# A four-layer trunk on one core: x's and h's two-part buffers each shifted in memory by an unused buffer

## The chip, the cores and the metric

The kernel runs on one core of one Trainium2 chip. The metric is the device time of one execution in microseconds (us). TensorE (PE) multiplies matrices, VectorE (DVE) and ScalarE (ACT) work element by element, GpSimd (POOL) has small jobs, and SyncE (SP) issues the DMAs that bring the weights in.

## What is computed

The reference is a trunk of four layers over 256 tokens of width 1024, all in 32-bit floats:

```
for i in range(DEPTH):                                # 4
    x = x + 0.5 * swiglu(rms_norm(x), gate, up, down) # 1024 -> 2816 -> 1024
    h = rms_norm(x)
    x = x + mixer[i % 3](h)      # fox attention, conv module, diff attention
    x = x + 0.5 * swiglu(rms_norm(x), gate, up, down)
```

swiglu is (silu(h @ w_gate) * (h @ w_up)) @ w_down. There are eight such blocks (called ffn below) and four mixers: fox, conv, diff, fox. All weights are read once; with them some 346 MB come from memory.

## The kernel before

Activations stand transposed: 128 features on the partitions, tokens along the row. A product of 32-bit numbers is made of three products of rounded parts (type float32r): each operand is split into a high part and the low rest, and high x high, high x low and low x high are summed in a PSUM bank.

Weights arrive in blocks of 128 partitions x 2048 floats (8 tiles k of 256 columns, 1024 bytes a tile) in a ring of 5 slots. ACT writes the high part (`split_high`, L468), DVE the low part (`split_low`, L786, in the memory where the block landed), and PE waits for the latter.

In an ffn the moving operand of a matmul has both parts side by side. `on_both` (L1362) streams the 256 high and the 256 low values of one tile of x or h (512 columns) past the high weights, and `on_high` (L1367) streams the 256 high values past the low weights. `both_parts` (L1370) issues, for one half n (128 columns) of the weight tiles: one L1362 for the first k, then L1367 for all k, then L1362 for the rest. Each such pair of matmuls, one L1362 and one L1367, handles one k and one n. Each matmul has its own weight load (LDWEIGHTS, in the rows PEld) of 128 columns, 512 bytes of a row.

- Gate and up: 11 pairs of blocks; each of the 22 blocks has 2 halves of 8 pairs of matmuls, so 352 pairs an ffn and 2816 in all, with x_both moving. x_both is [128, 2, 8, 256]: high tiles, then low tiles 8 KB on.
- Down: 12 blocks of 8, 8 and 6 tiles (`DOWN`), so 4 x 22 x 2 = 176 pairs an ffn and 1408 in all, with h_both moving. h_both is [128, 2, 22, 256]: low tiles 22 KB behind the high ones.
- Mixers: three matmuls of 256 columns (`three_passes`, L1353 to L1355), with x moving (`columns_half`), with x as the stationary operand and the weights moving (`tokens_half`), and with o_high and o_low moving (`rows_block`).

Buffers stand in a partition in the order of their declaration. In the built program the weights' ring starts at byte 16,512 (raw and, over it, w_low), w_high at 57,472, xT at 98,432, x_square at 106,624, x_both at 114,816, h_both at 177,376 (q_raw and u_shifted start there too, since they are alive at other times), o_high at 202,112 and o_low at 210,304. Called *phase* below is a byte address modulo 1024, and *distance* a buffer's phase less the weights'. Both parts of the weights have phase 128, and so has every tile of theirs; every tile of x_both has 128, of h_both 224, of o_high and o_low 384.

Of the kernel before, what the change touches and what calls it, by code (L numbers as in the profile page):

```python
# [14 lines left out]
P = 128  # L15
# [43 lines left out]
def build_trunk(nc, A, out):  # L59
# [12 lines left out]
    with ExitStack() as ctx:  # L72
        def sb(name, shape, dt=F32):
            return ctx.enter_context(nc.sbuf_tensor("sb_" + name, shape, dt))
# [10 lines left out]

        xT = sb("xT", [P, KT, SEQ])
        x_square = sb("x_square", [P, KT, SEQ])
        x_both = sb("x_both", [P, 2, KT, SEQ], F32R)
        x_high, x_low = x_both[:, 0, :, :], x_both[:, 1, :, :]
        square_sum = sb("square_sum", [P, SEQ])  # L90
# [64 lines left out]

        with ExitStack() as during_ffn:
            h_both = during_ffn.enter_context(nc.sbuf_tensor("sb_h_both", [P, 2, FF_TILES, SEQ], F32R))
            gate_part = during_ffn.enter_context(nc.sbuf_tensor("sb_gate_part", [P, 2, SEQ], F32))  # L160
            up_part = during_ffn.enter_context(nc.sbuf_tensor("sb_up_part", [P, 2, SEQ], F32))
# [1697 lines left out]
```

## Time and profile before

| what | value |
|---|---|
| median of 3 runs | 2031.18 us (2028.58 to 2031.52) |
| profiled execution, its own time | 2029.96 us |
| its span, first to last instruction | 2028.2 us |
| PE busy | 1986.3 us, 98% |
| DVE busy | 1425.3 us, 70% |
| ACT busy | 1045.6 us, 52% |
| memory traffic | 350.14 MB, 173 GB/s in the mean |
| granted TensorE clock, mean | 0.998 |

A matmul's end in the trace is modelled and lies past the start of the next, so the mean duration of one is no measure of how fast they follow each other. The pace is read from starts, or from the chain that ended last, which gives the time from one run of matmuls to the next.

### The profile page before, as it was taken

The numbers are of one execution on the slowest core, as the hardware profiler recorded it, in microseconds if no ns is written. First come the engines' busy times: TensorE is split into PE (matmuls) and PEld (weight loads), VectorE is DVE, ScalarE is ACT, GpSimd is POOL, SyncE is SP. The second block draws the span as 40 slices with busy tenths as digits, with TensorE's granted clock in tenths as the row PEclk, the third lists the DMA queues.
The fourth block names the chain that finished last, engine by engine and source line by source line (L and its number), as shares of the span: only waits on it lengthen the run. The fifth ranks groups of instructions, "written<-read, shape, count | busy, mean of one in ns | idle before, by whom it ended". The sixth has DMA issues, their size and how long they took to land.

```text
span 2028.2 us, 29077 instructions
## 1 busy us (share of the span) xinstructions
PE 1986.3 (98%) x12584; PEld 1744.9 (86%) x12584; DVE 1425.3 (70%) x1631; ACT 1045.6 (52%) x1247; POOL 114.2 (6%) x120
## 2 busy tenths in 40 slices
PE   7999999999999998999999999999999999999999
PEld 6888888888888896988888888888888888888887
DVE  7775777876787554776587658887658765778763
ACT  5544556654554344654465455665446545456542
POOL 2000201000200001100000000010010001101000
PEclk9999999999999999999999999999999999999999
DMA  7655433665665583565656553355566555335553
GB/s 226 192 183 178 146 125 121 196 193 176 193 190 186 180 248 88 182 190 183 193 187 192 174 181 125 111 181 187 177 197 187 187 184 171 125 114 177 187 183 109
DMA packets 336365, 350.14 MB, mean 173 GB/s; under 512 B 10077, under 2 KB 331886, under 8 KB 336238
## 3 DMA queue, kind: packets, MB, share of 16 engines
q1 hardware_dynamic: 331742, 343.58, 53.3%
q10 hardware_dynamic: 4496, 4.70, 1.0%
q8 instruction: 99, 1.62, 0.3%
q14 instruction: 28, 0.23, 0.0%
HBM read 346.04 MB, written 2.22 MB: 172 GB/s over the span
## 4 chain that ended last, share of the span: by engine, by line
PE 89%; DVE 5%; ACT 4%; issue 1%; DMA 1%; POOL 1%; ACTq 0%; DVEq 0%; POOLq 0%
PE banks L1362 48%; PE banks L1367 25%; PE banks L1353 4%; PE banks L1354 4%; PE banks L1355 4%; ACT sb_w_high L468 1%; DVE sb_w_low L786 1%; ACT sb_scores L594 1%; PE banks L1565 1%; PE banks L1795 1%; PE banks L1603 1%; DVE sb_neg_max L1053 0%; PE banks L1619 0%; PE banks L1586 0%; PE banks L1714 0%
## 5 line engine op out<-in xcount | busy, mean ns | idle before, releaser
L786 DVE TENSOR_TENSOR sb_w_low<-sb_raw,sb_w_high 128x2048 fp32r<-128x2048 f32 (+1 forms) x332 | 754.1, 2275 | 238.8 <-ACT sb_w_high L468 238.2
L1362 PE MATMUL banks<-sb_x_both,sb_w_high 128*128 128x512 f32 x2816 | 727.5, 394 | 3.4 <-DVE sb_w_low L786 3.4
L468 ACT ACTIVATE sb_w_high<-sb_raw 128x2048 fp32r<-128x2048 f32 (+1 forms) x332 | 618.7, 1867 | 141.2 <-DMA sb_raw<-in_ffn_w_down 112.0
L1362 PEld LDWEIGHTS banks<-sb_x_both,sb_w_high 128*128 128x128 f32 x2816 | 501.4, 189 | 86.1 <-DVE sb_w_low L786 3.8
L1367 PEld LDWEIGHTS banks<-sb_x_both,sb_w_low 128*128 128x128 f32 x2816 | 398.8, 191 | 36.0
L1367 PE MATMUL banks<-sb_x_both,sb_w_low 128*128 128x256 f32 x2816 | 408.6, 283 | 0.0
L1362 PE MATMUL banks<-sb_h_both,sb_w_high 128*128 128x512 f32 x1408 | 360.7, 395 | 0.0
L1362 PEld LDWEIGHTS banks<-sb_h_both,sb_w_high 128*128 128x128 f32 x1408 | 251.7, 188 | 46.6
L1367 PEld LDWEIGHTS banks<-sb_h_both,sb_w_low 128*128 128x128 f32 x1408 | 194.6, 188 | 17.1
L1367 PE MATMUL banks<-sb_h_both,sb_w_low 128*128 128x256 f32 x1408 | 200.3, 282 | 0.0
L486 ACT ACTIVATE sb_x_both<-sb_xT,sb_vec 128x256 fp32r<-128x256 f32 x96 | 43.5, 501 | 207.7 <-DVE sb_xT L819 179.1
L1353 PE MATMUL banks<-sb_x_both,sb_w_high 128*128 128x256 f32 x512 | 148.8, 291 | 0.0
L539 ACT ACTIVATE sb_up_part<-banks 128x512 f32<-128x512 f32 x88 | 52.3, 595 | 182.5 <-PE banks L1362 182.5
L1354 PE MATMUL banks<-sb_x_both,sb_w_high 128*128 128x256 f32 x512 | 144.9, 283 | 0.0
L1355 PE MATMUL banks<-sb_x_both,sb_w_low 128*128 128x256 f32 x512 | 144.8, 283 | 0.0
L539 ACT ACTIVATE sb_gate_part<-banks 128x512 f32<-128x512 f32 x88 | 52.4, 595 | 167.3 <-PE banks L1362 167.3
L952 DVE TENSOR_TENSOR sb_up_part<-banks,sb_up_part 128x512 f32<-128x512 f32 x88 | 60.7, 690 | 64.5 <-ACT sb_up_part L539 64.5
L1353 PEld LDWEIGHTS banks<-sb_x_both,sb_w_high 128*128 128x128 f32 x512 | 98.1, 192 | 3.2 <-issue 3.0
L1354 PEld LDWEIGHTS banks<-sb_x_both,sb_w_high 128*128 128x128 f32 x512 | 98.2, 192 | 1.6 <-issue 1.4
L936 DVE TENSOR_TENSOR sb_gate_part<-banks,sb_gate_part 128x512 f32<-128x512 f32 x88 | 60.7, 690 | 54.5 <-ACT sb_gate_part L539 54.2
L1355 PEld LDWEIGHTS banks<-sb_x_both,sb_w_low 128*128 128x128 f32 x512 | 98.1, 192 | 0.0
L816 DVE SCALAR_TENSOR_TENSOR sb_xT<-banks,sb_xT 128x512 f32<-128x512 f32 x32 | 22.1, 691 | 100.5 <-PE banks L1362 100.5
(210 smaller groups left out, 1957.1 us busy)
## 6 DMA issues: line engine op xcount, KB each, us to landing
sb_raw<-in_ffn_w_gate SPq DMA_DIRECT2D x88, 1024.0 KB, 5.4
sb_raw<-in_ffn_w_up SPq DMA_DIRECT2D x88, 1024.0 KB, 5.4
sb_raw<-in_ffn_w_down SPq DMA_DIRECT2D x64, 1024.0 KB, 5.0
sb_raw<-in_ffn_w_down SPq DMA_DIRECT2D x32, 768.0 KB, 4.3
sb_raw<-in_fox_w_in SPq DMA_DIRECT2D x24, 1024.0 KB, 5.2
sb_raw<-in_conv_w_pw SPq DMA_DIRECT2D x12, 1024.0 KB, 5.4
sb_raw<-in_diff_w_in SPq DMA_DIRECT2D x12, 1024.0 KB, 5.0
sb_raw<-in_fox_w_out SPq DMA_DIRECT2D x8, 1024.0 KB, 5.0
```

Source lines behind the costliest of these rows:

```text
L468: act.activation(slot(w_high, b)[:, 0:width(b)], slot(raw, b)[:, 0:width(b)], ACT.Copy).then_inc(S["high_ready"], 1)
L486: act.activation(x_high[:, t, :], xT[:, t, :], ACT.Copy, scale=vec[:, col + t:col + t + 1]).then_inc(S["xhigh_ready"], 1)
L539: act.activation((up_part if which else gate_part)[:, :, :], banks[:, at:at + 2, SEQ:], ACT.Copy).then_inc(S["up_part_ready" if which else ...
L786: dve.tensor_tensor(slot(w_low, b)[:, 0:width(b)], slot(raw, b)[:, 0:width(b)], slot(w_high, b)[:, 0:width(b)].bitcast(F32), ALU.subtract) ...
L816: dve.scalar_tensor_tensor(xT[:, 2 * T:2 * T + 2, :], sums[:, :, SEQ:], 0.5, xT[:, 2 * T:2 * T + 2, :], ALU.mult, ALU.add).then_inc(S["x_h ...
L936: dve.tensor_tensor(gate_part[:, :, :], banks[:, at:at + 2, 0:SEQ], gate_part[:, :, :], ALU.add).then_inc(S["gate_sum_ready"], 1)
L952: dve.tensor_tensor(up_part[:, :, :], banks[:, at:at + 2, 0:SEQ], up_part[:, :, :], ALU.add).then_inc(S["up_sum_ready"], 1)
L1353: pe.matmul(dst, s_high, m_high, start=first, stop=False, skip_group_check=loose)
L1354: pe.matmul(dst, s_high, m_low, start=False, stop=False, skip_group_check=loose)
L1355: return pe.matmul(dst, s_low, m_high, start=False, stop=last, skip_group_check=loose)
L1362: return pe.matmul(pair(bank[at][:, :]), high[:, n * P:(n + 1) * P], m_both, start=first, stop=last, skip_group_check=True)
L1367: pe.matmul(bank[at][:, SEQ:2 * SEQ], low[:, n * P:(n + 1) * P], m_high, start=False, stop=False, skip_group_check=True)
```

## The change

Two buffers are declared that nothing reads or writes.

```
         x_square = sb("x_square", [P, KT, SEQ])
+        sb("shift_x", [P, 16])
         x_both = sb("x_both", [P, 2, KT, SEQ], F32R)
...
+        sb("shift_h", [P, 200])
         with ExitStack() as during_ffn:
             h_both = during_ffn.enter_context(nc.sbuf_tensor("sb_h_both", [P, 2, FF_TILES, SEQ], F32R))
```

The first takes 16 floats = 64 bytes of each partition, the second 200 floats = 800 bytes. The weights, xT and x_square stay where they are. x_both and what is declared between it and h_both move up by 64 bytes, and h_both and what is declared behind it by 864. No instruction, wait, size or order differs.

## Rows read from the trace of the kernel before

**Rows 1.** Page: busy us by engine, and the granted clock in 40 slices.
```profile
PE 1986.3 (98%) x12584; PEld 1744.9 (86%) x12584; DVE 1425.3 (70%) x1631; ACT 1045.6 (52%) x1247; POOL 114.2 (6%) x120
...
PEclk9999999999999999999999999999999999999999
```

**Rows 2.** Page: the chain that ended last, by engine and by line.
```profile
PE 89%; DVE 5%; ACT 4%; issue 1%; DMA 1%; POOL 1%; ACTq 0%; DVEq 0%; POOLq 0%
PE banks L1362 48%; PE banks L1367 25%; PE banks L1353 4%; PE banks L1354 4%; PE banks L1355 4%; ACT sb_w_high L468 1%; DVE sb_w_low L786 1%; ACT sb_scores L594 1%; PE banks L1565 1%; PE banks L1795 1%; PE banks L1603 1%; DVE sb_neg_max L1053 0%; PE banks L1619 0%; PE banks L1586 0%; PE banks L1714 0%
```

**Rows 3.** Stretches, gate and up and down: PE, PEld, DVE, ACT, POOL, clock, DMA, GB/s.
```profile
836.00:906.00 70.00, 70.00 (x403) 61.62 (x402) 57.88 (x55) 42.11 (x43) 0.00 (x0) 1.00 0.63 199
951.00:1009.00 58.00, 58.00 (x331) 50.56 (x331) 30.72 (x24) 22.22 (x20) 3.70 (x5) 1.00 0.58 185
```

**Rows 4.** PE in order of time, gate and up: start us, length us (last end modelled), what.
```profile
874.00 2.00 PE L1362 MATMUL banks<-sb_x_both,sb_w_high 128*128 128x512 f32 x8
...
929.87 2.00 PE L1362 MATMUL banks<-sb_x_both,sb_w_high 128*128 128x512 f32 x8
```

**Rows 5.** Chain that ended last, 940 to 1010 us: start us, time to the next piece, what.
```profile
941.20 1.84 PE banks L1362 x8
943.04 0.95 PE banks L1367 x8
944.00 1.84 PE banks L1362 x8
...
956.87 0.96 PE banks L1367 x8
957.83 1.87 PE banks L1362 x8
959.70 0.72 PE banks L1367 x6
960.41 1.40 PE banks L1362 x6
```

**Rows 6.** The same chain over the whole span, its longest pieces: same down stage.
```profile
988.92 1.87 PE banks L1362 x8
```

**Rows 7.** PE in order of time: first matmul of a gate-and-up stage, of its down stage, of the next.
```profile
824.90 0.40 PE L1362 MATMUL banks<-sb_x_both,sb_w_high 128*128 128x512 f32 x1
...
948.24 0.40 PE L1362 MATMUL banks<-sb_h_both,sb_w_high 128*128 128x512 f32 x1
...
1010.41 0.39 PE L1362 MATMUL banks<-sb_x_both,sb_w_high 128*128 128x512 f32 x1
```

**Rows 8.** PE in order of time: o moving, 23 matmuls from the first start to the last.
```profile
321.29 0.28 PE L1354 MATMUL banks<-sb_o_low,sb_w_high 128*128 128x256 f32 x1
...
323.91 0.28 PE L1355 MATMUL banks<-sb_o_high,sb_w_low 128*128 128x256 f32 x1
```

**Rows 9.** PE in order of time: weights moving, x stationary, 7 matmuls.
```profile
299.51 0.28 PE L1355 MATMUL banks<-sb_w_high,sb_x_both 128*128 128x256 f32 x1
...
300.22 0.28 PE L1355 MATMUL banks<-sb_w_high,sb_x_both 128*128 128x256 f32 x1
```

**Rows 10.** PE in order of time, half clock, o moving, 10 matmuls.
```profile
799.91 0.42 PE L1355 MATMUL banks<-sb_o_high,sb_w_low 128*128 128x256 f32 x1
...
801.83 0.41 PE L1355 MATMUL banks<-sb_o_high,sb_w_low 128*128 128x256 f32 x1
```

**Rows 11.** Stretches of rows 10 and rows 8: busy us by engine, granted clock, DMA share, GB/s.
```profile
799.50:802.50 3.00, 3.00 (x15) 3.00 (x16) 1.33 (x2) 2.94 (x7) 0.00 (x0) 0.50 0.02 5
321.00:324.00 3.00, 3.00 (x28) 3.00 (x26) 2.76 (x11) 1.32 (x6) 0.00 (x0) 1.00 0.77 270
```

**Rows 12.** Weight loads by line and form, whole span: count, busy us, mean ns.
```profile
L1362 PEld LDWEIGHTS banks<-sb_x_both,sb_w_high 128*128 128x128 f32 x2816 | 501.4, 189 | 86.1 <-DVE sb_w_low L786 3.8
L1367 PEld LDWEIGHTS banks<-sb_x_both,sb_w_low 128*128 128x128 f32 x2816 | 398.8, 191 | 36.0
L1362 PEld LDWEIGHTS banks<-sb_h_both,sb_w_high 128*128 128x128 f32 x1408 | 251.7, 188 | 46.6
L1367 PEld LDWEIGHTS banks<-sb_h_both,sb_w_low 128*128 128x128 f32 x1408 | 194.6, 188 | 17.1
```

More of the change, by code:

```diff
@@ L87, in build_trunk @@
         x_square = sb("x_square", [P, KT, SEQ])
+        sb("shift_x", [P, 16])
         x_both = sb("x_both", [P, 2, KT, SEQ], F32R)
@@ L154, in build_trunk @@
         neg_lam = sb("neg_lam", [P, 1])
+        sb("shift_h", [P, 200])
         with ExitStack() as during_ffn:
```

## Prediction

> **What bounds the kernel now.** I read the page first. PE is busy 98% of the span and the clock is full nearly throughout [rows 1]; the chain of waits that ended last lies on PE for 89%, and 73 of these points are the two matmul lines of the ffn stages [rows 2]. DVE and ACT have room: in a stretch of gate and up PE is busy 70.00 of 70 us, DVE 57.88 and ACT 42.11; in a down stage 58.00 of 58, 30.72 and 22.22, with DMA engines at 0.58 to 0.63 [rows 3]. So in the ffn stages nothing but the pace of PE's own stream sets the time. The change moves data and nothing else; it can act only if that pace hangs on addresses.
>
> So the pace itself has to be read. Gate and up: two runs of eight L1362 start at 874.00 and 929.87 us; a run of eight L1362 and one of eight L1367 take about 2.79 us [rows 4, 5], so 20 such rounds or 160 pairs lie between, 349.2 ns a pair. Down: the same place of a round recurs at 957.83 and 988.92 us [rows 5, 6], two output tiles of 44 pairs apart, so 31.09 us / 88 = 353.3 ns a pair. The whole stages agree: 824.90 to 948.24 us for 352 pairs is 350.4 ns (with the sum of squares and the start in it), and 948.24 to 1010.41 for 176 is 353.2 [rows 7].
>
> The reader is to see that the same two instructions, with the same sizes, go 4.1 ns a pair slower with h moving than with x moving. The chain tells where: eight L1362 take 1.84 us with x and 1.87 with h, six take 1.40 with h (233 ns each against 230), while eight L1367 take 0.95 and 0.96 [rows 5]. DVE and ACT are less busy in the slower stage [rows 3], so it is not they. Three things differ: h stands at distance 96 from the weights and x at 0; h starts at a multiple of 32 bytes (177,376) but not of 64, x at a multiple of 128 (114,816); and h's low part lies 22 KB behind its high part, x's 8 KB.
>
> **What the pace holds beyond the columns.** At half clock (1.2 GHz), 9 starts of 256-column matmuls take 801.83 - 799.91 = 1.92 us, 213.3 ns each, which is 256 columns at that clock and nothing more [rows 10, 11]. At full clock (2.4 GHz) the columns would take half, 106.7 ns; 22 starts with o moving take 2.62 us, 119.1 ns each [rows 8, 11]. So each matmul holds about 12 ns more than its columns. A pair has 768 columns, 320 ns, and takes 349.2 or 353.3: 29 or 33 ns of something else. Part of this might be two streams of reads, the running matmul's data and the next weights, getting into each other's way at certain addresses. That is all that this change could win.
>
> **What the rows say of addresses.** 256-column matmuls go at 119 ns with o at distance 256 [rows 8], at 0.95/8 = 119 with x at distance 0, at 0.96/8 = 120 with h at 96 [rows 5], and at 0.71/6 = 118 with the roles of x and weights exchanged [rows 9]. Weight tiles are read in halves 512 bytes apart, and the chain's runs of eight L1362 with x at one half and at the next take 1.84 us both [rows 5]. So for these four distances the short matmul does not care. Only the 512-column matmul shows a difference, and only for h.
>
> **The change part by part.** No instruction comes or goes, so there is no count to price, only paces.
>
> h_both: 177,376 + 864 = 178,240, phase 64, distance -64. It becomes a multiple of 64 bytes, as x is. My reading is that the start of a row of h off a multiple of 64 makes each 256-value run touch one more unit of memory, which the 512-column matmul, with two such runs, pays and the short one hides. Then h falls to x's pace: 353.3 - 349.2 = 4.1 ns x 1408 pairs = 5.8 us. Bounds: nothing, if the 22 KB or something else is the cause; and more than 5.8 only if distance itself matters (a rival below).
>
> x_both: 114,816 + 64 = 114,880, phase 192, distance 64. Still a multiple of 64, no longer of 128. The trace has nothing at distance 64 or at an odd multiple of 64, so this is the term that I can't read. From both sides: above, x falls to h's pace, +4.1 x 2816 = +11.5 us; below, the 29 ns vanish, -29 x 2816 = -82 us. I take 0, because distances 0 and 256, both multiples of 64, give one pace for the short matmul, and the only deviating buffer is the one that is not such a multiple.
>
> Mixers: x moving there moves by 64, o by 864 to distance 96. Their short matmuls go at 119 at 0 and 256, and h's at 120 at 96: 768 matmuls with o x 0.5 ns is 0.4 us at most. I take 0. What else moves (scores, probabilities, padded conv input, copies that DVE, ACT and POOL read and write) moves by 64 or 864 bytes under operations that lie beside PE's work in all but a few per cent of the chain [rows 2]; 0 as well. If every DVE and ACT piece on the chain, 9% of it, changed by 1%, that would be 1.8 us either way.
>
> Sum: -5.8 us. Against the profiled execution 2028.2 - 5.8 = 2022.4 us of span, its own time 2029.96 - 5.8 = 2024.2; that execution is 1.2 us under the median. From the median of the runs: 2031.2 - 5.8 = **2025.4 us**, -0.29%. What a measurement of this kernel tells from no change is about 0.2%, 4.1 us.
>
> **A rule against it.** L1367's weight loads last 191 ns in the mean beside x and 188 beside h [rows 12], so loads are, if anything, shorter beside the slower stream; the trace alone does not decide whether the two streams meet. The Trainium skill (TensorE: Matmul & The Clock Gate, Step-by-step: what each phase is for) says that PE has two independent read ports and that loading the next weights takes nothing from the running matmul. By that rule distance is nothing, and the sum would be 0 for it. The Trainium skill (SBUF — State Buffer, Door 1: The DMA port swizzle) also says that memory lines are 16 bytes; by that rule an address off 64 but on 32 costs nothing, the sum is 0 again, and no row at a finer offset can show it.
>
> **The rivals.**
>
> *Addresses do nothing.* h's 4.1 ns come of its 22 KB between parts, which stays. For it: one pace at distances 0, 256 and 96 for short matmuls [rows 5, 8]. Against it: nothing in the trace ties 22 KB to a cost either. Time: 2031 us. Chance 0.23. The two rules of the Trainium skill cited above speak for this rival; the second is from its page SBUF — State Buffer.
>
> *x gets slower.* The unit is 128 bytes and not 64, or a small distance that is not 0 costs, as 96 does. x's rows start at 64 past a multiple of 128 and go at h's pace; h stays at its own. Place: every L1362 of gate and up. Price: +4.1 x 2816 = +11.5 us, 2042.7 us, +0.57%. It decides once x loses more than h's 5.8 us / 2816 = 2.1 ns a pair. For it: the only distance between 0 and 256 in the trace is the slow one. Against: the short matmul at 96 is as fast as the others. Chance 0.27.
>
> *The streams come apart.* At 64 bytes from the weights the reads of matmul and weights never meet, and some of the 29 to 33 ns a pair goes. All of it would be 29 x 2816 + 33 x 1408 = 128 us, 1903 us; a sixth of it 21 us, 2010 us. For it: the 12 ns that each matmul holds at full clock and none at half clock [rows 8, 10]. Against: halves of the weight tiles 512 bytes apart are served alike, and 0, 96 and 256 hold the same 12 ns; a meeting that only one distance avoids should show a trace at these. Chance 0.12.
>
> *Other*, such as both streams worse than any shown distance: 0.05, mostly slower.
>
> **How the numbers follow.** My forecast has the remaining 0.33; its own range is 2022 to 2031, since h may keep some of its difference. Of it I count 0.24 as faster by over 0.2% and 0.09 as within. Of the first rival 0.02, 0.19 and 0.02 are faster, within and slower, for scatter between runs. Of x slower, 0.24 slower and 0.03 within, if h gains at the same time (+5.7 net, near the bound). The third rival gives 0.12 faster, the rest 0.01 and 0.04. Sum: faster 0.39, within 0.31, slower 0.30. The range holds forecast, no effect, x slower and the mild part of the third rival: 2012 to 2044 us. It leaves out most of the third rival and what is worse than 2044.
>
> **What would show each step.** In the profile after, down rounds 88 pairs apart by 30.7 us and eight L1362 in 1.84 us, with gate and up still at 2.79 us a round: right as forecast. Down still at 31.09: addresses do nothing for h. Gate and up at 2.83 us a round: x slower. Rounds under 2.75 us in either: streams come apart. PE's busy share stays at 98% in every case. The prediction is wrong if the pace of x moves at all, since twice as many pairs hang on it as on h's.

## The result and the profile after

The changed kernel takes 2008.4 us (median of 4 runs, 2007.77 to 2009.38) against 2030.62 beside it; the ratio is 0.9894, 95% interval 0.9882 to 0.9906. It is 1.06% or some 22 us faster, 3.6 us below the range that was given (2012 to 2044 us).

The page of the changed kernel (busy us by engine; two lines more in the source, so L1362 is L1364 and L1367 is L1369) shows the same bound as [rows 1]: PE busy 98% with 25.8 us less, DVE and ACT unchanged.

```profile
span 2006.3 us, 29077 instructions
...
PE 1960.5 (98%) x12584; PEld 1722.1 (86%) x12584; DVE 1424.5 (71%) x1631; ACT 1045.4 (52%) x1247; POOL 114.2 (6%) x120
```

The first matmuls of a gate-and-up stage, its down stage and the next, changed kernel, answer to [rows 7] (start us, modelled length, what):

```profile
816.38 0.40 PE L1364 MATMUL banks<-sb_x_both,sb_w_high 128*128 128x512 f32 x1
...
938.15 0.40 PE L1364 MATMUL banks<-sb_h_both,sb_w_high 128*128 128x512 f32 x1
...
999.46 0.39 PE L1364 MATMUL banks<-sb_x_both,sb_w_high 128*128 128x512 f32 x1
```

Gate and up takes 121.77 us for 352 pairs, 345.9 ns a pair, where it took 350.4; down takes 61.31 us for 176, 348.3 where it took 353.2. Gate and up is 123.34 - 121.77 = 1.57 us shorter and down 62.17 - 61.31 = 0.86; in eight ffn these are 12.6 us with x and 6.9 us with h, 19.4 us together by the unrounded paces. The span is 2028.2 - 2006.3 = 21.9 us shorter, which leaves some 2.5 us for the rest, the mixers among it. That rest is one profiled execution less another, and ten executions of one kernel lay 4.8 us apart (2026.62 to 2031.38 us, the kernel with everything moved, below), so it is no more than a hint.

The chain that ended last, changed kernel, answers to [rows 5] (start us, time to the next piece, what):

```profile
931.20 1.83 PE banks L1364 x8
933.03 0.94 PE banks L1369 x8
933.97 1.83 PE banks L1364 x8
935.81 0.91 PE banks L1369 x8
936.71 1.83 PE banks L1364 x8
...
947.60 1.86 PE banks L1364 x8
949.46 0.69 PE banks L1369 x6
950.14 1.40 PE banks L1364 x6
```

The reader is to see where the time went out. With x moving (down to 936.71), eight long matmuls lost only 0.01 us, 1.84 to 1.83. Eight short ones went from 0.95 to 0.94 and 0.91 in turn: the two halves of a weight tile, alike before, are now served at different paces. With h moving (from 947.60), six long ones take 1.40 as before and six short ones 0.69 instead of 0.72. Of the 4.5 ns a pair with x and the 4.9 with h, most sits in the short matmuls, of which the prediction said that they do not care.

The weight loads answer to [rows 12] (view of groups by line; count, busy us, mean ns): beside x, the load of low weights is now 188 ns in the mean where it was 191.

```profile
L1369 PEld LDWEIGHTS banks<-sb_x_both,sb_w_low 128*128 128x128 f32 x2816 | 391.2, 188 | 36.8
```

### The profile page after: what moved, and what is told of

It is laid out like the page before. It is cut to its first block, busy times and chain, and to the rows that moved or that the text cites. A ratio compares the mean times of both kernels' runs of the same rounds, so it can differ in the third digit from the quotient of the medians.

```text
span 2006.3 us, 29077 instructions
## 1 busy us (share of the span) xinstructions
PE 1960.5 (98%) x12584; PEld 1722.1 (86%) x12584; DVE 1424.5 (71%) x1631; ACT 1045.4 (52%) x1247; POOL 114.2 (6%) x120
## 4 chain that ended last, share of the span: by engine, by line
PE 88%; DVE 5%; ACT 4%; issue 2%; DMA 1%; POOL 1%; ACTq 0%; DVEq 0%; POOLq 0%
PE banks L1364 48%; PE banks L1369 24%; PE banks L1355 4%; PE banks L1357 4%; PE banks L1356 4%; ACT sb_w_high L470 1%; DVE sb_w_low L788 1%; ACT sb_scores L596 1%; PE banks L1567 1%; PE banks L1797 1%; DVE sb_neg_max L1055 1%; PE banks L1605 0%; PE banks L1716 0%; DVE sb_scores L1048 0%; DMA u_away<-sb_u_pad 0%
## 5 line engine op out<-in xcount | busy, mean ns | idle before, releaser
L1364 PE MATMUL banks<-sb_x_both,sb_w_high 128*128 128x512 f32 x2816 | 723.0, 392 | 3.5 <-DVE sb_w_low L788 3.5
L1364 PEld LDWEIGHTS banks<-sb_x_both,sb_w_high 128*128 128x128 f32 x2816 | 497.7, 188 | 82.9 <-DVE sb_w_low L788 3.9
L1369 PEld LDWEIGHTS banks<-sb_x_both,sb_w_low 128*128 128x128 f32 x2816 | 391.2, 188 | 36.8
L1369 PE MATMUL banks<-sb_x_both,sb_w_low 128*128 128x256 f32 x2816 | 399.5, 278 | 0.0
L1364 PE MATMUL banks<-sb_h_both,sb_w_high 128*128 128x512 f32 x1408 | 360.1, 394 | 0.0
L1364 PEld LDWEIGHTS banks<-sb_h_both,sb_w_high 128*128 128x128 f32 x1408 | 250.2, 188 | 45.7
L1369 PEld LDWEIGHTS banks<-sb_h_both,sb_w_low 128*128 128x128 f32 x1408 | 190.8, 188 | 17.1
L1369 PE MATMUL banks<-sb_h_both,sb_w_low 128*128 128x256 f32 x1408 | 194.3, 279 | 0.0
L1355 PE MATMUL banks<-sb_x_both,sb_w_high 128*128 128x256 f32 x512 | 146.7, 286 | 0.0
L1357 PE MATMUL banks<-sb_x_both,sb_w_low 128*128 128x256 f32 x512 | 142.8, 279 | 0.0
L1356 PE MATMUL banks<-sb_x_both,sb_w_high 128*128 128x256 f32 x512 | 142.7, 279 | 0.0
L1355 PEld LDWEIGHTS banks<-sb_x_both,sb_w_high 128*128 128x128 f32 x512 | 96.1, 188 | 3.2 <-issue 3.0
L1356 PEld LDWEIGHTS banks<-sb_x_both,sb_w_high 128*128 128x128 f32 x512 | 96.2, 188 | 1.7 <-issue 1.4
L1357 PEld LDWEIGHTS banks<-sb_x_both,sb_w_low 128*128 128x128 f32 x512 | 96.0, 188 | 0.0
```

Of the source, the lines that this page charges most:

```text
L1355: pe.matmul(dst, s_high, m_high, start=first, stop=False, skip_group_check=loose)
L1356: pe.matmul(dst, s_high, m_low, start=False, stop=False, skip_group_check=loose)
L1357: return pe.matmul(dst, s_low, m_high, start=False, stop=last, skip_group_check=loose)
L1364: return pe.matmul(pair(bank[at][:, :]), high[:, n * P:(n + 1) * P], m_both, start=first, stop=last, skip_group_check=True)
L1369: pe.matmul(bank[at][:, SEQ:2 * SEQ], low[:, n * P:(n + 1) * P], m_high, start=False, stop=False, skip_group_check=True)
```

## The experiments

Distances are those of the front part: phase of a buffer less that of the weights, in bytes modulo 1024. Paces are read as above, from the same three starts in the middle of the kernel (gate and up / 352, down / 176), each from one profiled execution. They repeat to 0.3 ns from stage to stage of one execution, but for the first gate and up and the first and last down, which hold other work or waits. Where only one execution of a kernel was timed, its time can be some us off, and the paces are the measure. All shifts are multiples of 32 bytes, so finer distances were not tried. The weights start at a multiple of 64 bytes in every kernel, so the distances 32, 96, 160 and 224 are also those at which the moving buffer starts off a multiple of 64.

**x alone.**

```
+        sb("shift_x", [P, 16])     # ahead of x_both: x at 64
+        sb("shift_h", [P, 240])    # ahead of h_both: moved by 1024 in all, h stays at 96, o at 256
```

> Only x's part is kept: 64 unused bytes ahead of x_both, and 960 ahead of h_both, so that h, o and all that stands behind them move by a whole kilobyte and keep their phase (h at distance 96, o at 256). Theory D (the pace hangs on the distance of the moving operand from the weights within a kilobyte): gate and up as in the changed kernel, 345.7 ns a pair, down as before, 353.25 ns; the mixers' matmuls with x moving at 117 ns, with o moving at 119.8. Sum: 2030.6 less the 12.3 us that gate and up gave and about 2.5 of the mixers, 2016 us. Theory A (the pace hangs on where a buffer starts modulo 64 or 128, whatever the weights do) expects the same here. Rival C (what moved beside x and h made the gain): 2030.

2016.22 us (4 runs), ratio 0.9939 (0.9922 to 0.9956). Its stages start at 819.81, 941.67 and 1003.86 us: 346.2 ns a pair with x, 353.3 with h: x takes its gain alone, and h's move by a whole kilobyte does nothing.

**h alone.**

```
+        sb("shift_h", [P, 216])    # 864 bytes ahead of h_both, nothing ahead of x_both
```

> Only h's part: 864 unused bytes ahead of h_both, none ahead of x_both. h at distance -64, o at 96, x at 0. Theory D and theory A: down at 348.3 ns a pair, gate and up at 350.1 as before; 2030.6 less 7.0 = 2023.6 us. Rival C: no such split; the stages of down would stay at 353.25.

2023.13 us (6 runs), ratio 0.9966 (0.9954 to 0.9979). Stage starts at 824.04, 947.37 and 1008.66 us: 350.4 and 348.3 ns a pair. The two parts, 0.61% and 0.34%, add up to 0.95%; both together gave 1.06%, and the intervals are wide enough for that. In paces each part is alone what it is beside the other, to 0.3 ns: x's is 346.2 alone and 345.9 with h's move, h's 348.3 in both. Rival C of the expectations (something moved beside x and h) is out for the ffn stages.

**All moved together.**

```
+        sb("shift_all", [P, 16])   # ahead of the weights and all else
```

> 64 unused bytes ahead of everything, the weights too: all distances stay as they were before (x 0, h 96, o 256), while all addresses move by 64, so that x starts at 64 modulo 128 as in the changed kernel. Theory D: as before, 2030.6 us, 350.1 and 353.25 ns a pair. Theory A: gate and up at 345.7 ns a pair, 2016 to 2018 us.

2028.89 us (10 runs), ratio 0.9999 (0.9990 to 1.0009). Its stages, beside [rows 7]:

```profile
824.97 0.40 PE L1363 MATMUL banks<-sb_x_both,sb_w_high 128*128 128x512 f32 x1
...
948.32 0.40 PE L1363 MATMUL banks<-sb_h_both,sb_w_high 128*128 128x512 f32 x1
...
1010.49 0.39 PE L1363 MATMUL banks<-sb_x_both,sb_w_high 128*128 128x512 f32 x1
```

123.35 and 62.17 us, as before to 0.01 us, though x starts at the very byte where it starts in the changed kernel, 114,880. Where x starts by itself does not matter; the distance from the weights is what counts. This decides against theory A for x. It says nothing against the prediction's reading of h: h starts off a multiple of 64 here too (177,440). A kernel with everything moved by 32 bytes would try that alone, and there is none.

**The two distances exchanged.**

```
+        sb("shift_x", [P, 240])    # x at -64
+        sb("shift_h", [P, 8])      # h at +64, o at 224
```

> The two distances exchanged: x at -64, h at +64 (960 unused bytes ahead of x_both, 32 ahead of h_both). Theory D in its simple form (two streams that must not read the same place at once; the moving operand is read twice as fast as the weights): which half of a weight tile suffers is exchanged, the sums stay near the changed kernel, 2007 to 2012 us. If only the lead of the moving operand helps, x loses its gain and the time is near 2022. Theory A: as the changed kernel, 2008.4, since both buffers start at 64 modulo 128.

2005.27 us (4 runs), ratio 0.9882 (0.9866 to 0.9899). Stage starts at 815.29, 937.80 and 998.70: x 348.1 ns a pair, h 346.0. The sign matters: for both buffers +64 is the faster side, by 2.2 and 2.3 ns. x keeps half of its gain, so neither "sums stay" nor "only the lead helps" is quite right. By these paces the kernel should be slower than the changed one by 2.2 x 2816 - 2.3 x 1408 = 3.0 us, yet its profiled span is 0.5 us shorter (the intervals of the two ratios overlap), and its time is below the 2007 us of the expectation. What it gained lies outside the ffn stages, where o stands at 224 instead of 96 and its matmuls are busy 2.2 us less in sum; what the rest is was not traced.

**The curve.** Four kernels with other sizes of the same two unused buffers, one execution each, tell a single meeting in a kilobyte (K) from a shorter period (R).

```
shift_x  32 bytes, shift_h none: x  32, h 128
shift_x 128 bytes, shift_h 992:  x 128, h 192
shift_x 256 bytes, shift_h 32:   x 256, h 384
shift_x 512 bytes, shift_h 416:  x 512, h 0
```

> A point of the curve of pace over distance: x at 32, h at 128 (o at 288). Theory K (one meeting: the next weights, 512 bytes at half the speed of the moving data, are met by it once per load only in some halves; period a kilobyte): x at 32 nearly as at 64, 346 to 347 ns a pair, h at 128 as at +64, 346.0. Theory R (what counts is the distance modulo 128: 0 slow, 64 fast, between them uneven): x at 32 between, 347 to 351, h at 128 slow, 350 or more. Span 2005 to 2012 by K, 2020 or more by R.

> x at 128, h at 192 (o at 352). Theory K: both as at 64, 345.8 and 346.0 ns a pair, span near 2002. Theory R: x as at 0, 350.1, h as at 64, 346.0, span near 2018.

> x at 256, h at 384 (o at 544). Theory K: 345.8 and 346.0 ns a pair. Theory R: 350.1 and near 350. The runs with o moving at distance 256 (119.8 ns a matmul, as x at 0) speak for R.

> x at 512, h at 0 (o at 160). Both theories: x as at 0, 350.1 ns a pair, since weight halves stand 512 bytes apart. h at 0: if the distance is all that parts x's pace from h's, h takes x's pace of before, about 349.5 ns a pair; if the 22 KB between h's parts count for themselves, h stays at 351 or more.

Times 2024.99, 2026.11, 2023.76 and 2024.57 us, the kernel before beside them 2030.83. K is wrong: x at 128 goes at 352.2 ns a pair, slower than at 0, where K had 345.8. R has 0, 256 and 512 right but not 128, which it puts at the pace of 0; and h at 192 goes at 348.2, not at 346.0. The stages of the third kernel (x 256, h 384) start at 821.21, 944.54 and 1006.39 us: 123.33 / 352 = 350.4 ns at 256, the pace of distance 0. The fourth gives 350.4 for x at 512 (starts 823.46 and 946.79) and, with the next stage at 1008.28, 61.49 / 176 = 349.4 for h at 0. h at 0 is thus no slower than x at 0, and the 22 KB between h's parts cost nothing that can be seen.

**Two more points of the curve.**

```
shift_x 160 bytes, shift_h 32:   x 160, h 288 (32 modulo 256)
shift_x  96 bytes, shift_h 32:   x  96, h 224
```

> x at 160, h at 288 (32 modulo 256), o at 448 (192). P256: h as x at 32, 350.7 ns a pair or a little less; x at 160 not yet seen, between 346 and 353.

> x at 96, h at 224, o at 384 (128 modulo 256). P256 and the blind prediction alike: x at 96 goes as h did there before, 353 ns a pair, so gate and up lose 8 us or more against 350.1. h at 224 not yet seen; o at 224 gave 118.3 ns a short matmul, so between 347 and 350.

2027.28 and 2039.01 us, one execution each, before 2027.97 in the median. The second is the slowest kernel of the study, 0.5% over before. Its stages:

```profile
828.80 0.39 PE L1364 MATMUL banks<-sb_x_both,sb_w_high 128*128 128x512 f32 x1
...
953.60 0.39 PE L1364 MATMUL banks<-sb_h_both,sb_w_high 128*128 128x512 f32 x1
...
1015.40 0.40 PE L1364 MATMUL banks<-sb_x_both,sb_w_high 128*128 128x512 f32 x1
```

124.80 / 352 = 354.5 ns with x at 96, the distance at which h went at 353.2 before. All points together, by distance modulo 256 (in brackets the distance where it is another):

| distance mod 256 | x moving, ns a pair | h moving, ns a pair |
|---|---|---|
| 0 | 350.4; 350.4 (256); 350.4 (512) | 349.4 |
| 32 | 351.0 | 350.6 (288) |
| 64 | 345.9 to 346.2 | 346.0; 345.8 (320) |
| 96 | 354.5 | 353.2 |
| 128 | 352.2 | 351.3; 351.4 (384) |
| 160 | 352.2 | |
| 192 | 348.1 (960) | 348.2; 348.3 (960) |
| 224 | | 351.1 |

Wherever two distances equal modulo 256 were tried the paces agree to 0.3 ns, and x and h follow one curve to 1.3 ns (x's stage also holds a sum of squares, L1417 before). It has a low at 64, a smaller one at 192, a high at 96, and is not smooth: 64 and 96, 32 bytes apart, are its two ends. A start off a multiple of 64 does not sort these paces: 32 and 224 (351.0, 350.6, 351.1) are off it and no slower than 128 (352.2, 351.3), which is on it.

**What meets the moving data: w_high 64 bytes off w_low.**

```
+        sb("shift_w", [P, 16])     # between w_low and w_high; x at 64 from w_low, at 0 from w_high
```

> 64 unused bytes between w_low and w_high and none elsewhere: x is at 64 from w_low and at 0 from w_high (h at 160 and 96). Each matmul runs while the weights of the next are loaded, low weights during a run of L1367-like matmuls, high ones during a run of L1362-like ones. Theory L (what meets the moving data is the load of the next weights): eight short matmuls of gate and up in a row take 906 or 944 ns by half, as with x at 64, and eight long ones 1840, as with x at 0; about 347.6 ns a pair. Rival: the meeting is with something else that stands ahead of x (xT, x_square, w_low as the memory into which DMA and DVE write): then short and long matmuls change together, to 350.1 or to 345.8 ns a pair.

```
+        sb("shift_w", [P, 16])     # between w_low and w_high
+        sb("shift_x", [P, 16])     # x at 128 from w_low, at 64 from w_high
```

> 64 unused bytes between w_low and w_high and 64 ahead of x_both: x is at 64 from w_high and at 128 from w_low. Theory L (the load of the next weights is what meets): runs of eight long matmuls as with x at 64, 1828 and 1834 ns, runs of eight short ones as with x at 128, 942 and 954 ns; pair about 347.5 ns. If history between the runs counts as well, as the first kernel of this kind suggests, both come out between their own pure values and those of the other distance.

2021.40 and 2026.23 us, one execution each. Chain that ended last, first of the two (x at 64 from w_low, 0 from w_high):

```profile
927.23 1.82 PE banks L1363 x8
929.05 0.94 PE banks L1368 x8
929.99 1.86 PE banks L1363 x8
931.85 0.94 PE banks L1368 x8
```

and of the second:

```profile
927.89 1.84 PE banks L1364 x8
929.73 0.96 PE banks L1369 x8
```

Neither is what theory L said. In the first the long runs average 1.84 as said, but differ by half, and the short ones take 0.94 in both halves where 0.91 and 0.94 were due. In the second the long ones take 1.84 instead of 1.83, and the short ones 0.96 in both halves (also those that start at 926.93 and 932.53 us), more than at either pure distance. Nor is it only the ends of a run, where a short matmul stands beside a long one: the third to the seventh step from start to start in a run of eight short ones is 117.8 and 118.1 ns by half in the first kernel, against 113.9 and 117.3 in the changed one, though x is at 64 from w_low in both. So runs of one kind do not have a pace of their own; the other kind counts as well. The pair gives 349.0 in the first, between the values for its two distances (350.4, 346.1) and nearer the first, and 351.3 in the second, where the pure ones are 352.2 and 346.1. Theory L had said 347.6 and 347.5.

**The same with all weight loads from w_high.** These two leave out the low weights in the ffn stages: the short matmul loads high weights. w_low is still written.

```
-                    on_high(at, n, low[:, k, :], m_both(k)[:, 0, :])
+                    on_high(at, n, high[:, k, :], m_both(k)[:, 0, :])
```

In the first, w_high is 64 bytes off w_low and x at 0 from w_high; in the second, `shift_x` of 64 bytes alone puts x at 64 from both.

> Leaves out the low weights in the ffn stages: the short matmuls load the high weights instead, so every weight load there reads w_high; w_low is still written. w_high is 64 bytes off w_low, x at 0 from w_high and at 64 from w_low. Theory L (only what PE loads counts): gate and up exactly as before, 350.1 ns a pair, runs of eight 952 and 1840. Rival (writes of DMA and DVE into w_low count, or w_low's place by itself): as the last split kernel, 348.7, or 345.8.

> The same without low weights in the ffn stages, w_high not moved, x at 64 from both, h at 160. Control of the last: gate and up as in the changed kernel, 345.8 ns a pair, runs of eight 906 or 944 and 1828 or 1834; down as x at 160, near 351.5.

2027.12 and 2011.17 us, one execution each. The first:

```profile
823.41 0.40 PE L1363 MATMUL banks<-sb_x_both,sb_w_high 128*128 128x512 f32 x1
...
946.75 0.40 PE L1363 MATMUL banks<-sb_h_both,sb_w_high 128*128 128x512 f32 x1
...
1008.92 0.39 PE L1363 MATMUL banks<-sb_x_both,sb_w_high 128*128 128x512 f32 x1
```

350.4 and 353.2 ns a pair: the kernel before to the digit, with w_low at another distance and DMA and DVE writing into it all the while. The first kernel of the section before has the same layout and differs only in that its short matmuls load from w_low; it goes at 349.0 and 350.4. The second gives 346.1 with x (starts 817.46, 939.29), near the changed kernel's pace, and with the next start at 1001.17 us 351.6 with h at 160, where x gave 352.2. So what counts is the distance between what a matmul streams and the weights that PE itself loads. The place of w_low counts for nothing where PE does not load from it.

**A better version.**

```
+        sb("shift_x", [P, 16])     # x at 64
+        sb("shift_h", [P, 40])     # 160 bytes: h at 320, 64 modulo 256; o at 480
```

> The candidate for a better version: 64 unused bytes ahead of x_both, 160 ahead of h_both, so that x stands at 64 and h at 320, which is 64 modulo 256. The runs so far gave x the same pace at 0, 256 and 512 (350.1 ns a pair) and h the same at 128 and 384 (351.3, 351.4) and at 192 and -64 (348.2, 348.3), so the period should be 256 bytes. Theory P256: gate and up as in the changed kernel, 345.7 ns, down at 346.0 as h at +64; against the changed kernel 2.3 ns x 1408 = 3.2 us less in down, and some 3 us less in the mixers, where o at 480 (224 modulo 256) should go at 118.3 ns as in the mirrored kernel: 2003 us. Rival K (one meeting in a kilobyte): h at 320 would differ from h at 64.

2002.56 us (4 runs), ratio to before 0.9876 (0.9857 to 0.9896). Its stages start at 813.86, 935.62 and 996.48 us: 121.76 us with x as in the changed kernel and 60.86 with h instead of 61.31, 0.45 us in each of eight down stages or 3.6 us in all. The spans differ by 2006.3 - 2001.4 = 4.9 us. The two kernels were not timed against each other; against the kernel before, the intervals of the two ratios overlap. So the gain in down is shown by the paces, and that of the whole kernel is not clear of the scatter.

```
+        sb("shift_o", [P, 24])     # the last, and 96 bytes ahead of o_high: o at 64 modulo 256
```

> The better version so far (x at 64, h at 320, which is 64 modulo 256) with 96 more unused bytes ahead of o_high, so that o stands at 64 modulo 256 too instead of 224. By the curve a short matmul with o moving goes at 115 to 117 ns instead of 118.3: 768 of them, 1 to 2.5 us less than 2002.6, so 2000 to 2001.5 us.

2002.63 us (4 runs), ratio 0.9865 (0.9849 to 0.9882), span 2002.0 against 2001.4. The 1 to 2.5 us for o did not show; what o gives lies under the scatter.

## Why the prediction was wrong, step by step

*PE's own pace sets the time, and the change acts only through addresses*: right. Busy share, DVE, ACT and the number of instructions are the same, and 19.4 of the 21.9 us come out of the two stages whose time that stream sets.

*h: 4.1 ns a pair, 5.8 us*: measured 4.9 ns and 6.9 us, but the runs don't bear out the reason. The reading was that h pays for not starting at a multiple of 64. Off such a multiple h also goes at 350.6 and 351.1, and on one at 351.3 (distances 288, 224 and 128), so this is not what parts fast from slow. What goes with its pace is the distance of 96, the slowest of the curve for x too (354.5). That a start off a multiple of 64 has a part in it at 96 is not excluded, since the two never came apart. That the forecast came out near is luck: h was sent to 192 modulo 256, which is 348.3, and not to 349.4, its pace at x's old distance.

*x: 0*: this is the step that failed. Gate and up fell by 4.5 ns a pair, from 350.4 to 345.9, which is 12.6 of the 16 us that were missing. It was said that the trace has nothing at distance 64 and that distances 0 and 256, both multiples of 64, give one pace. They do, since the curve's period is 256: 0, 256 and 512 are one point of it, seen three times. From it a flat curve was read between points that could not have differed. The distance of 96, the only other point, was put down to something else.

*The short matmul does not care for distance*: wrong, and by the same aliasing. It was read at 0, at 256, at halves 512 apart, and at 96, where it goes as at 0 (0.96 and 0.95 for eight). At 64 it takes 0.94 and 0.91, and this is most of the gain: about 0.025 us a run of eight, against 0.01 for the long ones.

*The mixers: 0*: the two stages leave 2.5 us over. The short matmuls with x moving in the mixers follow the same distance: the 512 of L1354 were busy 144.9 us (283 ns in the mean) and are 142.7 (279) as L1356, and the other two lines of 512 lose about as much, some 6 us of busy time in all. Less than half of it shows in the span. PE also waits for ACT and DVE in the mixers, which may take up the rest; that was not traced, and 2.5 us lies within the scatter.

*The rivals.* "Addresses do nothing" is refuted, and h's 22 KB cost nothing that can be seen (349.4 with h at 0). Between the fastest and the slowest distance of x lie 8.6 ns of 354.5. The Trainium skill (TensorE: Matmul & The Clock Gate, Step-by-step: what each phase is for) says that the next weights' load takes nothing from the running matmul. What the prediction drew from it, that distance is nothing, is wrong here; whether it is the load that takes those 8.6 ns is left open below. "The streams come apart" had the right sign and kind, with a chance of 0.12, but is right in part only: 4.5 to 4.9 ns of the 29 to 33 beyond the columns went. Its own sign, rounds of gate and up under 2.75 us, shows in every other round only: they last 2.77 and 2.74 us in turn (starts 931.20, 933.97 and 936.71). "x gets slower" is what a distance of 96 or 128 does, up to 4.1 ns a pair as priced, and 32 by 0.6; it is true of the neighbours of 64 and not of 64. The range stopped 2 us above what a sixth of the third rival would give (2010 us), and about a sixth of it is what came: 19.4 us of 128.

*What stays open.* At the best distance a pair still takes 345.8 ns for 320 ns of columns; whether the remaining 26 ns can be had at any address is not known. That the running matmul meets the load of the next weights in time was not shown as such: shown is that the place from which PE loads counts, and that short and long runs influence each other. Whether a start off a multiple of 64 has a part at the distances 32, 96, 160 and 224 was not tried by itself. Why the curve has its shape is not known, and its value between the steps of 32 bytes was not measured.

## What to carry to other kernels

Where PE is busy from end to end, read the pace of one matmul from starts, compare it with its columns, and compare stages that run the same instructions on different buffers: a difference of a few ns between them may be an address. Before reading "no dependence" from points of a trace, ask with what period they might coincide, and take a sweep of a few unused buffers to settle it; here a few unused bytes moved the time between 2039 and 2002.6 us. An unrelated buffer declared ahead of an operand can change the time of a kernel by 1%, and a comparison of two versions should keep operands and weights at the same distance.

## What the runs showed of the hardware

Matmuls of type float32r (256 or 512 columns, a new load of 128 columns for each) pace by the distance between moving data and loaded weights with a period of 256 bytes: 345.9 ns a pair at 64, 354.5 at 96, 350.4 at 0, 256 and 512. Moving all buffers by 64 bytes together changes nothing (350.4 and 353.2 as before). The pace repeats to 0.3 ns from stage to stage of one execution, and the place of w_low, into which the DMAs and DVE write, does not change it where PE does not load from there (350.4 with x at 0 and at 64 from w_low). And runs of short and long matmuls act on each other: with high and low weights at different distances, eight short ones take 0.96 us, against 0.94 and 0.91 at distance 64 and 0.94 and 0.95 at 128.
